# The last expert's second layer in column halves, and the last LayerNorm's affine passes moved from GpSimd to VectorE

## The reference, cut to what matters

```python
def expert_block(args):
    xb, e = args
    hid = xb @ lp["moe_w1"][e] + lp["moe_b1"][e]          # 1024 -> 2048
    gate = jnp.minimum(hid[:, :D_FF], SWIGLU_LIMIT)
    lin = jnp.clip(hid[:, D_FF:], -SWIGLU_LIMIT, SWIGLU_LIMIT)
    act = gate * jax.nn.sigmoid(SWIGLU_ALPHA * gate) * (lin + 1.0)
    return act @ lp["moe_w2"][e] + lp["moe_b2"][e]        # 1024 -> 1024
...
out = layer_norm(DEEPNORM_ALPHA * h + moe(h, lp), lp["ln2_g"], lp["ln2_b"])
```

## Time and profile before

| what | value |
|---|---|
| median of 3 runs | 1108.36 us (1108.23 to 1110.98) |
| the profiled execution: its own time | 1107.56 us |
| its span, first to last instruction | 1105.8 us |
| mean granted TensorE clock | 0.997 |
| TensorE matmul busy | 1068.5 us, 97% |
| VectorE busy | 374.0 us, 34% |
| ScalarE busy | 163.6 us, 15% |
| GpSimd busy | 44.3 us, 4% |
| HBM read | 423.39 MB, 385 GB/s over the span |

### The profile page before, as it was taken

The page is one execution under the profiler, slowest core; times in us unless marked ns, Lnnn a source line. Parts: engine busy times, 40 slices in busy tenths (PEclk is TensorE's granted clock), DMA queues, the critical chain, the costliest instruction groups (busy, mean ns, idle before and its releaser), DMA issues.

```text
span 1105.8 us, 13963 instructions
## 1 busy us (share of the span) xinstructions
PE 1068.5 (97%) x5411; PEld 461.6 (42%) x5411; DVE 374.0 (34%) x939; ACT 163.6 (15%) x314; POOL 44.3 (4%) x103
## 2 busy tenths in 40 slices
PE   7999999999999999999999999999999999999896
PEld 4667554434343433334343333333333333434332
DVE  4697665223231313131414141313232323122134
ACT  4164623000100000001000100010101010100002
POOL 8000310000000000000000000000000000000001
PEclk9999999999999999999999999999999999999998
DMA  9534649999999999999999999999999999999993
GB/s 297 196 142 165 250 161 366 403 425 428 430 427 426 427 429 429 430 427 428 429 430 430 427 428 428 429 430 428 428 427 430 429 430 427 427 429 429 428 426 151
DMA packets 41790, 425.77 MB, mean 385 GB/s; under 512 B 6633, under 2 KB 13166, under 8 KB 17177
## 3 DMA queue, kind: packets, MB, share of 16 engines
q1 hardware_dynamic: 39873, 423.62, 91.4%
q0 software_dynamic: 1888, 1.75, 0.6%
HBM read 423.39 MB, written 2.17 MB: 385 GB/s over the span
## 4 chain that ended last, share of the span: by engine, by line
PE 76%; DMA 21%; DVE 2%; issue 0%; ACT 0%; SPq 0%; DVEq 0%
PE bank L1922 34%; DMA ring<-in_moe_w_dram 21%; PE bank L1937 11%; PE bank L1524 7%; PE bank L1883 6%; PE bank L1896 6%; PE bank L1751 3%; PE bank L1781 2%; PE bank L1551 1%; PE bank L1947 1%; PE bank L1529 1%; PE bank L1891 1%; PE bank L1995 0%; PE bank L1773 0%; PE bank L1744 0%
## 5 line engine op out<-in xcount | busy, mean ns | idle before, releaser
L1922 PE MATMUL bank<-ring,hT 128*64 128x512 f32 x2048 | 455.4, 595 | 16.1 <-DMA ring<-in_moe_w_dram 16.1
L1922 PEld LDWEIGHTS bank<-ring,hT 128*64 128x64 f32 x2048 | 141.5, 137 | 301.0 <-issue 267.1
L1937 PE MATMUL bank<-ring 128*64 128x512 f32 x1024 | 227.0, 595 | 0.7 <-DMA ring<-in_moe_w_dram 0.7
L1416 DVE TENSOR_SCALAR ring<-bank 128x512 f32<-128x512 f32 x32 | 22.1, 692 | 312.2 <-PE bank L1922 312.2
L1937 PEld LDWEIGHTS bank<-ring 128*64 128x64 f32 x1024 | 70.6, 137 | 133.8 <-issue 126.6
L1433 DVE COPY ring<-bank 64x512 f32<-64x512 f32 x32 | 22.2, 694 | 219.9 <-PE bank L1937 219.9
L1883 PEld LDWEIGHTS bank<-ring 128*128 128x128 f32 x744 | 85.4, 192 | 25.2 <-issue 25.2
L1883 PE MATMUL bank<-ring 128*128 128x128 f32 x744 | 91.3, 279 | 0.0
L1365 DVE TENSOR_SCALAR hT<-bank,ring 128x128 f32<-128x128 f32 x128 | 43.6, 402 | 130.9 <-PE bank L1883 130.4
L906 ACT ACTIVATE ring<-ring 128x512 f32<-128x512 f32 x32 | 20.1, 630 | 380.8 <-DVE ring L1416 380.8
L1896 PE MATMUL bank<-ring 128*128 128x512 f32 x128 | 63.5, 618 | 0.0
(11 more groups left out here) (327 smaller groups left out, 618.1 us busy)
## 6 DMA issues: line engine op xcount, KB each, us to landing
ring<-in_moe_w_dram SPq DMA_DIRECT2D x192, 2048.0 KB, 29.5
ring<-in_w_in_dram SPq DMA_DIRECT2D x5, 1536.0 KB, 13.5
ring<-in_w_out_dram SPq DMA_DIRECT2D x2, 2048.0 KB, 11.0
ring<-in_w_in_dram SPq DMA_DIRECT2D x1, 2048.0 KB, 13.2
xt<-in_x_prompt_dram SPq DMA_DIRECT2D x2, 512.0 KB, 3.8
lnbc<-in_ln_g_dram SPq DMA_DIRECT2D x2, 512.0 KB, 12.2
lnbc<-in_ln_b_dram SPq DMA_DIRECT2D x2, 512.0 KB, 12.6
out_dram<-xt SPq DMA_DIRECT2D x4, 256.0 KB, 2.1
```

Source lines behind the costliest of these rows:

```text
L1922: ins = pe.matmul(bank[b][64 * h:64 * h + 64, :], xT[:, q, k, j * CAP:(j + 1) * CAP], ring[:, c:c + 512], start=False, stop=k == KT - 1)
L1937: ins = pe.matmul(bank[OUT_BANK[j]][64 * h:64 * h + 64, :], actT[:, j, k % 4, (k // 4) * CAP:(k // 4 + 1) * CAP], ring[:, c:c + 512], star ...
```

## The change

The second layer of the very last expert is computed in this order: half 0 for all eight k, half 1 for k 0 to 3, then the sample's sums of half 0 and the sums of chunks 0 and 2 (the first halves of both prompt tiles), then half 1 for k 4 to 7. The remaining sums (sample columns of half 1, chunks 1 and 3) follow after the last copy. Residuals 2 and 3 are put in with 0 and 1, before the second layer of the pair's first expert. In every pair VectorE now copies both halves of expert 0 and ScalarE both halves of expert 1; a new semaphore `out_half` tells that half 0 of expert 1 is done. The four affine passes of prompt tile 0 are all done by VectorE, behind everything else; GpSimd keeps the two for the sample. VectorE takes the statistics of chunks 0 and 2 first, and makes the sample's scale and shift after the variance of tile 1. ScalarE's tail is as it was. Stores of tile 0 wait for `y_done[0]` in turn.

```diff
-LAST_ORDER = (4, 0, 1, 2, 3)
+LAST_ORDER = (0, 2, 4, 1, 3)
...
-            sp.wait_ge(y_done[0], 1)
-            sp.dma_start(y_prompt[0, 0:P, 0:512], Y[:, 0, 0:512]).then_inc(out_stored, 16)
-            sp.wait_ge(y_done[3], 1)
-            sp.dma_start(y_prompt[0, 0:P, 512:D], Y[:, 0, 512:D]).then_inc(out_stored, 16)
+            for h in range(2):
+                sp.wait_ge(y_done[0], h + 1)
+                sp.dma_start(y_prompt[0, 0:P, h * 512:(h + 1) * 512], Y[:, 0, h * 512:(h + 1) * 512]).then_inc(out_stored, 16)
...
-            pool.wait_ge(ld_ln, 96)
-            pool.wait_ge(y_hat, 1)
-            st.then(pool.tensor_tensor(Y[:, 0, 0:512], Y[:, 0, 0:512], ln2[:, 0, 0:512], ALU.mult))
-            st.do(pool.tensor_tensor(Y[:, 0, 0:512], Y[:, 0, 0:512], ln2[:, 1, 0:512], ALU.add), y_done[0])
...
-                        for j in range(2):
-                            act.wait_ge(w_used, PAIR * pi + 2 * W1P + 2 * j + 2)
-                            act.activation(eout[64 * j:64 * j + 64, 0, :], bank[OUT_BANK[j]][0:64, :], ACT.Copy
-                                           ).then_inc(out_ready, 1)
+                        act.wait_ge(out_half, pi + 1)
+                        act.activation(eout[64:128, 0, :], bank[OUT_BANK[1]][0:64, :], ACT.Copy).then_inc(out_ready, 1)
+                        act.wait_ge(w_used, PAIR * pi + PAIR)
+                        act.activation(eout[64:128, 1, :], bank[OUT_BANK[1]][64:128, :], ACT.Copy).then_inc(out_ready, 1)
...
-                        def expert_out(j):
-                            dve.wait_ge(w_used, PAIR * pi + 2 * W1P + 2 * j + 2)
-                            dve.tensor_copy(eout[64 * j:64 * j + 64, 1, :], bank[OUT_BANK[j]][64:128, :]).then_inc(out_ready, 1)
+                        def expert_out():
+                            dve.wait_ge(w_used, PAIR * pi + 2 * W1P + 2)
+                            for h in range(2):
+                                dve.tensor_copy(eout[0:64, h, :], bank[OUT_BANK[0]][64 * h:64 * h + 64, :]).then_inc(out_ready, 1)
...
+            def gained(h):
+                w = slice(h * 512, (h + 1) * 512)
+                dve.wait_ge(y_hat, h + 1)
+                st.do(dve.tensor_tensor(Y[:, 0, w], Y[:, 0, w], ln2[:, 0, w], ALU.mult))
+            def offset(h):
+                w = slice(h * 512, (h + 1) * 512)
+                st.do(dve.tensor_tensor(Y[:, 0, w], Y[:, 0, w], ln2[:, 1, w], ALU.add), y_done[0])
+            half_stats(0, 0)
+            half_stats(1, 0)
             dve.wait_ge(last_summed, LAST_ORDER.index(4) + 1)
             st.do(dve.bn_stats(sq6[:, :], bank[LAST_BANK[4]][:, 0:QD]), sample_stats)
-            half_stats(0, 0)
+            half_stats(0, 1)
             dve.wait_ge(sample_moved, 4)
             variance(2, SAMP, s46[0:SAMP, :, :])
-            half_stats(0, 1)
             st.settle()
             variance(0, P, stat[:, 0, :, :])
-            scale_and_shift(2, SAMP, 0)
-            half_stats(1, 0)
-            scale_and_shift(0, P, 1)
             half_stats(1, 1)
             st.settle()
             variance(1, P, stat[:, 1, :, :])
+            scale_and_shift(2, SAMP, 0)
+            scale_and_shift(0, P, 1)
             dve.wait_ge(ld_ln, 96)
             minus_mean(0)
...
-            w1 = slice(512, D)
-            dve.wait_ge(y_hat, 2)
-            st.then(dve.tensor_tensor(Y[:, 0, w1], Y[:, 0, w1], ln2[:, 0, w1], ALU.mult))
-            st.do(dve.tensor_tensor(Y[:, 0, w1], Y[:, 0, w1], ln2[:, 1, w1], ALU.add), y_done[3])
+            gained(0)
+            gained(1)
+            st.settle()
+            offset(0)
+            offset(1)
...
+            def add_sample(q0, q1):
+                for q in range(q0, q1):
+                    ins = pe.matmul(bank[LAST_BANK[4]][SAMP * q:SAMP * q + SAMP, 0:QD], putT[:, 2 * P:2 * P + SAMP],
+                                    eout[:, q // 2, (q % 2) * QD:(q % 2 + 1) * QD], start=False, stop=True)
+                return ins
+            def add_experts(c):
+                pe.matmul(bank[LAST_BANK[c]][:, :], putT[:, c // 2 * P:(c // 2 + 1) * P], eout[:, c % 2, :], start=False, stop=True
+                          ).then_inc(last_summed, 1)
...
+                def second_step(j, f, k, h):
+                    c = f % 4 * 2 * SLOT + k * D + h * 512
+                    return pe.matmul(bank[OUT_BANK[j]][64 * h:64 * h + 64, :],
+                                     actT[:, j, k % 4, (k // 4) * CAP:(k // 4 + 1) * CAP],
+                                     ring[:, c:c + 512], start=k == 0, stop=k == KT - 1)
...
+                            ins = second_step(j, f, k, h)
+                            if j == 1 and k == KT - 1 and h == 0:
+                                ins.then_inc(out_half, 1)
...
+                def last_half(f, k0, k1):
+                    for k in range(k0, k1):
+                        ins = second_step(1, f, k, 1)
+                        if k % 4 == 3:
+                            ins.then_inc(w_used, 1)
+                def last_layer():
+                    f = (PAIR * q + 2 * W1P + 2) // 2
+                    for k in range(KT):
+                        if k == 0:
+                            pe.wait_ge(w_full[f % 4], 16 * (gi * 3 + f // 4 + 1))
+                        if k == 4:
+                            pe.wait_ge(w_half[f % 4], 16 * (gi * 3 + f // 4 + 1))
+                        ins = second_step(1, f, k, 0)
+                    ins.then_inc(out_half, 1)
+                    last_half(f, 0, 4)
+                    pe.wait_ge(out_ready, n_pass * (4 * PAIRS))
+                    add_sample(0, 2)
+                    add_experts(0)
+                    add_experts(2)
+                    last_half(f, 4, KT)
...
                     residual(0)
                     residual(1)
+                    pe.wait_ge(g1_ready, 2 * pi + 2)
+                    residual(2)
+                    pe.wait_ge(l1_ready, 2 * pi + 2)
+                    residual(3)
...
-                second_layer(1, 0, KT)
+                if final:
+                    last_layer()
+                else:
+                    second_layer(1, 0, KT)
...
-            pe.wait_ge(g1_ready, n_pass * NE)
-            pe.wait_ge(l1_ready, n_pass * NE)
-            residual(2)
             pe.wait_ge(out_ready, n_pass * (4 * PAIRS) + 1)
-            add_experts(4)
-            add_experts(0)
+            add_sample(2, 4).then_inc(last_summed, 1)
             add_experts(1)
-            add_experts(2)
-            residual(3)
             add_experts(3)
```

More of the change, by code:

```diff
@@ L360, in build_kernel @@
         putT_full, putT_ready = sem("putT_full"), sem("putT_ready")
-        out_ready = sem("out_ready")
+        out_ready, out_half = sem("out_ready"), sem("out_half")
         comb_full, y_added = sem("comb_full"), sem("y_added")
@@ L365, in build_kernel @@
         rows_normed, sample_normed = sem("rows_normed"), sem("sample_normed")
-        y_done = [sem(f"y_done{n}") for n in range(4)]
+        y_done = [sem(f"y_done{n}") for n in range(3)]
         ld_lnq = sem("ld_lnq")
@@ L1448, in _ @@
                         batch_out(1 - q, 0)
-                        expert_out(0)
-                        expert_out(1)
+                        expert_out()
             def half_stats(t, c):
```

## The result

| | before | after |
|---|---|---|
| median | 1108.52 us (1108.23 to 1110.98, 4 runs) | 1115.74 us (1115.58 to 1117.83, 4 runs) |
| ratio | | 1.0068, 95% interval 1.0056 to 1.0080 |
| span of the profiled execution | 1105.8 us | 1116.0 us |
| first residual of the last pair | 1070.14 | 1073.25 |
| from there to the end of the span | 35.6 | 42.8 |

A forecast was written before the change was run, and what follows sets the result against it. TensorE's matmul side, busy 97% of the span, was taken as the bound. The terms 8.0 - 0.1 + 0 - 0.05 gave +7.85 us: 1107.56 profiled becomes 1115.4, as median 1116.2, range 1113.5 to 1118.5.

The forecast's parts named there:

- What one product costs: TensorE: a product's two records cost 0.86 us alone, 0.43 beside a partner; a lone record costs what a pair does.
- Rivals 1 and 2: Lone records in halves: weight loads show, +12 us, chance 0.04; or a lone narrow product costs half, +3.7, chance 0.05.
- Second layer in halves: Last expert's second layer on TensorE: 9.43 us instead of 3.43 after the last weights land, 6.0 us more.
- rival 3: Last expert's second layer: engine runs half 1 beside half 0 by itself; whole change +1.7 us, 1110, chance 0.04.
- pairs of records in the halves' stretch: Sign of being wrong, last expert's second layer: records paired, where 32 single ones 0.43 us apart were forecast.
- Sums in between: TensorE before half 1's k 4 to 7: sample's sums free beside half 1's last product, chunks 0 and 2 cost 2.0 us.
- Last copy: Layer's end to first product on `eout`: ScalarE's copy of 0.59 replaces VectorE's 0.69, 0.1 us less than 1.15.
- The tail: First product on the last copy to VectorE's last pass's end: 12.1 us against 12.15, gains given back.
- the added wait: In the tail, VectorE idles some 1.3 us before the reciprocal, for ScalarE's root, as the sample's scale and shift come later.
- Every pair: Copies dealt out anew and the extra semaphore in all pairs: cost nothing; at most 9 us if the cover were gone.
- Residuals 2 and 3: 1.72 us of products moved into TensorE's idle time behind residuals 0 and 1: 0, bounds 0 and 0.15.
- Last pass to the end: VectorE's last pass to the end of the span: 3.25 us, carried over unchanged from the kernel before.

The follow-up runs named there:

- blocks8: Kernel before, with only the last expert's second layer as half 0 for all eight k, then half 1, no sums in between: 1113.42 us, 1.0052.
- blocks4: Kernel before, with only the last expert's second layer alternating between halves in blocks of four k-steps: 1110.28 us, 1.0014.
- blocks2: Kernel before, with only the last expert's second layer alternating between halves in blocks of two k-steps: 1108.88 us, 1.0002.
- best_a: Kernel before, with GpSimd's two passes on tile 0 given to VectorE and residuals 2 and 3 put in with 0 and 1: 1107.38 us, 0.9988.
- after_early_shift: Changed kernel, with the sample's scale and shift ahead of the last statistics again and tile 0's behind them: 1114.37 us, 1.0051 against the kernel before.
- after_pairs: Changed kernel, with the last expert's second layer in pairs again and all sums behind the last copy: 1110.19 us, 1.0008 against the kernel before.
- after_gpsimd: Changed kernel, with half 0 of tile 0 given back to GpSimd as two passes: 1116.32 us, 1.0069 against the kernel before.
- before_no_gpsimd: Kernel before, with only GpSimd's two passes on half 0 of tile 0 moved to VectorE: 1107.50 us, 0.9991.

## Why the prediction was right

1116.2 us was forecast with 1113.5 to 1118.5, slower; 1115.7 was measured, and +7.85 us forecast became +7.2. The main mechanism, lone products at the full price of a step, is right. That the sum came out this close is in part luck: four steps are off by 0.4 to 0.8 us each, two too dear and two too cheap. By its steps:

The steps begin at k-step 4 of half 0, 1088.93 in the changed kernel; a layer's part ends 0.43 behind the start of its last record (1093.70 and 1099.75).

| step, us | forecast | measured |
|---|---|---|
| last weights to the end of half 1, k 3 | 6.0 | 1094.13 - 1088.93 = 5.2 |
| sums in between | 1.97 | 1096.69 - 1094.13 = 2.56 |
| half 1, k 4 to 7 | 3.43 | 3.49 |
| layer's end to the first product on the last copy | 1.05 | 1101.03 - 1100.18 = 0.85 |
| from there to the end of the last pass | 12.1 | 1113.51 - 1101.03 = 12.48 |
| last pass to the end of the span | 3.25 | 2.5 |

*What one product costs* held: 0.43 a step for a narrow record alone, with the load hidden. The rule of the Trainium skill weighed there (TensorE: Matmul & The Clock Gate, Part 3, loads overlap only with another row group) did not: the lone loads of 0.14 lie inside steps of 0.43. Rivals 1 and 2 are out.

*Second layer in halves* was 0.8 too dear: the step "its first product can go beside the last one of half 0" should have said the last two. This is rival 3 in small: the engine does run half 1 beside half 0 by itself, but for one product further only. The prediction named pairs of records in the halves' stretch as a sign of being wrong, and four steps had them. The Trainium skill's sentence in the same section that products start and end strictly in program order is contradicted by the changed kernel and by blocks8, blocks4 and blocks2. What nothing here shows is how a queue of other shapes or of shorter products behaves.

*Sums in between* was 0.6 too cheap. The sample's two products did not go beside the last product of half 1, though they use the other columns; they start 0.09 after its last step has ended. Their wait on `eout`, long fulfilled, stands between, and so does a change of shape (32 columns and 256 moving elements after 64 and 512). A fulfilled wait alone does not forbid the overlap: in blocks4, k-step 4 of half 0 waits for weights that have landed, and still its loads fall in one step with one of half 1 (timeline of PEld, blocks4), as the 20 steps require:

```profile
1090.14 0.19 PEld L1954 LDWEIGHTS bank<-ring 128*64 128x64 f32 x3 [0.29 <-issue]
```

Whether the change of shape does was not tried.

*Last copy* was 0.2 better than forecast. The 1.15 us of before were read as the copy and a fixed way behind it; best_a shows that residual 2, on TensorE between the layer and the sums, held the product back by 0.19. With the residual moved the product starts 0.05 behind ScalarE's copy (1100.38 + 0.59 to 1101.03). So moving residual 2 was a small gain, and not nothing.

*The tail* was right in its main point, that what it gains it gives back, and the added wait was 1.13 for 1.3. The stretched pass (0.48) was missing. Not the later scale and shift of the sample put it there, since it is 1.23 in after_early_shift too. In both kernels VectorE comes to the reciprocal no later than ScalarE's root, so its next pass and GpSimd's second one both follow ScalarE's chain and start 0.04 apart; before, VectorE had one statistics pass more between the sample's shift and the reciprocal than in after_early_shift, and came to it 0.5 us behind the root. The prediction also read the 1.75 of before as beside GpSimd's pass of 1.77; that pass ended at 1099.61, and the 1.75, from 1100.08 on, ran beside the next one.

*Every pair* and the place that *Residuals 2 and 3* were moved to cost nothing, as forecast: the +1.8 us of after_pairs are all in the last pair and the norm (37.53 - 35.64 = 1.9), and the changed kernel's lag of 3.3 us in the first expert is 3.1 at the last pair.

*Last pass to the end* was the step that failed outright: the 3.25 us of before were carried over as fixed. In truth GpSimd's drain held the end, and the change takes it off: 0.76 us of gain that no sentence named.

## What to carry to other kernels

Two narrow products that use different column groups of the array shared their time where at most one other product that had still to start stood between them. Finishing one group first gives the other engines their data early, but nearly doubles TensorE's time for that layer (28 steps for 16); in this shape blocks of two k-steps were free, blocks of four or eight were not. Before an epilogue is reordered, list what each engine does in order and when it closes: a small step moved back on one engine can hold another's whole queue, and an engine with a slow close should get its last work early.

## What the runs showed of the hardware that was not expected

- A product of this shape (64 columns, 512 moving elements, float32) could start ahead of one that stood before it in the program, one and no more: 28, 20 and 16 steps in blocks of 8, 4 and 2.
- GpSimd's closing drain ended 4.3 us after its last pass in the kernel before, the changed one, after_gpsimd and before_no_gpsimd, and ended the program of before 0.76 us late.
- In the norm, a VectorE pass with two operands from SBUF that started while a GpSimd pass (TENSOR_TENSOR) ran ended some 0.55 us after that pass, with 0.43 to 1.19 us of it left: it looks like a wait for its end, not like a shared rate. A pass that started ahead of GpSimd's kept its length: 0.75 at 1097.73 in the kernel before, with GpSimd's pass of 1.77 from 1097.84 on. The pass that reads a bank (L1467) took 0.75 beside one too, in after_early_shift and before_no_gpsimd. From the timelines of DVE and POOL:

| kernel | GpSimd's pass | VectorE's pass | its length | ends behind GpSimd's |
|---|---|---|---|---|
| before | 1097.84 to 1099.61 | 1099.18 to 1100.15 | 0.97 | 0.54 |
| before | 1099.68 to 1101.27 | 1100.08 to 1101.83 | 1.75 | 0.56 |
| changed | 1108.26 to 1108.98 | 1108.30 to 1109.53 | 1.23 | 0.55 |
| after_early_shift | 1107.22 to 1107.94 | 1107.26 to 1108.49 | 1.23 | 0.55 |
| after_gpsimd | 1106.37 to 1108.09 | 1107.65 to 1108.62 | 0.97 | 0.53 |
| after_gpsimd | 1108.16 to 1109.75 | 1108.56 to 1110.31 | 1.75 | 0.56 |
